# Shared memory region at a multiple of 128 bytes, step sizes computed behind the convolution, first transfers in another order

## What is computed

```python
def mamba2_mixer(u, w_in, conv_w, conv_b, dt_bias, a_log, d_skip, norm_g, w_out):
    b, l, _ = u.shape
    zxbcdt = u @ w_in
    z, xbc, dt = jnp.split(zxbcdt, [D_INNER, D_INNER + CONV_DIM], axis=-1)
    xbc = lax.conv_general_dilated(
        xbc, conv_w[:, None, :].astype(xbc.dtype), window_strides=(1,),
        padding=[(D_CONV - 1, 0)], dimension_numbers=('NWC', 'WIO', 'NWC'),
        feature_group_count=CONV_DIM)
    xbc = jax.nn.silu(xbc + conv_b)
    xs, bm, cm = jnp.split(xbc, [D_INNER, D_INNER + SSM_GROUPS * D_STATE], axis=-1)
    dt = jax.nn.softplus(dt.astype(jnp.float32) + dt_bias.astype(jnp.float32))
    a = -jnp.exp(a_log.astype(jnp.float32))
...
    y = ssd_chunked(xs, dt.reshape(b, l, SSM_GROUPS, SSM_HPG), a.reshape(SSM_GROUPS, SSM_HPG),
...
    y = y.reshape(b, l, D_INNER) * jax.nn.silu(z.astype(jnp.float32))
    y = grouped_rmsnorm(y, norm_g)
    return y.astype(u.dtype) @ w_out
```

## Time and profile before

| | us |
|---|---|
| three runs | 981.8, 981.83, 982.46 |
| median | 981.83 |
| profiled execution | 982.02 |
| its span, first to last instruction | 980.2 |
| mean granted TensorE clock | 0.983 of 2.4 GHz |
| TensorE busy | 927.5 (95%) |
| VectorE busy | 562.7 (57%) |
| ScalarE busy | 487.9 (50%) |
| read from memory | 162.01 MB, 166 GB/s over the span |

### The profile page before, as it was taken

The page is one execution under the profiler, slowest core; times in us unless marked ns, Lnnn a source line. Parts: engine busy times, 40 slices in busy tenths (PEclk is TensorE's granted clock), DMA queues, the critical chain, the costliest instruction groups (busy, mean ns, idle before and its releaser), DMA issues.

```text
span 980.2 us, 15470 instructions
## 1 busy us (share of the span) xinstructions
PE 927.5 (95%) x6560; PEld 855.4 (87%) x6560; DVE 562.7 (57%) x644; ACT 487.9 (50%) x669; POOL 37.3 (4%) x52
## 2 busy tenths in 40 slices
PE   2899998998999999999999999999999599999996
PEld 2899997876899889999988899997898499999885
DVE  4778654784475475455544755765654645554533
ACT  4555747773464564443343644665645534444332
POOL 1000001220000000000000021000000000000000
PEclk9899999998999999999999999999999799999999
DMA  9465553223464265555555697433543445555551
GB/s 294 141 194 187 172 173 109 88 86 131 170 221 166 86 215 172 178 195 183 172 188 198 197 275 236 131 129 123 198 152 98 139 133 193 188 171 175 201 181 43
DMA packets 120917, 163.80 MB, mean 167 GB/s; under 512 B 4060, under 2 KB 106644, under 8 KB 120868
## 3 DMA queue, kind: packets, MB, share of 16 engines
q1 hardware_dynamic: 117396, 151.47, 47.4%
q0 software_dynamic: 3472, 11.63, 4.0%
HBM read 162.01 MB, written 1.07 MB: 166 GB/s over the span
## 4 chain that ended last, share of the span: by engine, by line
PE 85%; DVE 7%; ACT 3%; DMA 2%; issue 2%; SPq 0%; POOL 0%; DVEq 0%
PE bank L433 77%; DMA w_raw<-in_ssm_w_in_dram 2%; DVE w_lo L1110 2%; DVE ntmp L1171 1%; PE bank L713 1%; PE bank L684 1%; DVE x L1174 1%; PE bank L533 1%; DVE ntmp L1150 1%; ACT ntmp L822 1%; PE bank L610 1%; PE bank L768 1%; DVE stats L1139 0%; DVE stats L1141 0%; PE bank L758 0%
## 5 line engine op out<-in xcount | busy, mean ns | idle before, releaser
L1110 DVE TENSOR_TENSOR w_lo<-w_raw,w_hi 128x2048 fp32r<-128x2048 f32 x136 | 310.8, 2290 | 229.2 <-ACT w_hi L802 229.1
L433 PE MATMUL bank<-actT_hi,w_hi 128*128 128x256 f32 x1280 | 365.5, 286 | 4.7 <-DVE dtc L1217 2.0
L433 PE MATMUL bank<-actT_lo,w_hi 128*128 128x256 f32 x1280 | 363.8, 284 | 0.0
L433 PE MATMUL bank<-actT_hi,w_lo 128*128 128x256 f32 x1280 | 363.6, 284 | 0.0
L802 ACT ACTIVATE w_hi<-w_raw 128x2048 fp32r<-128x2048 f32 x136 | 258.7, 1907 | 118.3 <-DMA w_raw<-in_ffn_w_down_dram 54.8
L433 PEld LDWEIGHTS bank<-actT_hi,w_hi 128*128 128x128 f32 x1280 | 247.3, 193 | 6.5 <-issue 4.2
L433 PEld LDWEIGHTS bank<-actT_lo,w_hi 128*128 128x128 f32 x1280 | 247.4, 193 | 0.1
L433 PEld LDWEIGHTS bank<-actT_hi,w_lo 128*128 128x128 f32 x1280 | 247.3, 193 | 0.0
L433 PE MATMUL bank<-w_lo,hT_hi 128*128 128x512 f32 x176 | 70.2, 399 | 0.0
L433 PE MATMUL bank<-w_hi,hT_hi 128*128 128x512 f32 x176 | 69.4, 394 | 0.0
L433 PE MATMUL bank<-w_hi,hT_lo 128*128 128x512 f32 x176 | 69.0, 392 | 0.0
(11 more groups left out here) (208 smaller groups left out, 1300.7 us busy)
## 6 DMA issues: line engine op xcount, KB each, us to landing
w_raw<-in_ffn_w_gu_dram SPq DMA_DIRECT2D x44, 1024.0 KB, 5.1
w_raw<-in_ffn_w_down_dram SPq DMA_DIRECT2D x22, 1024.0 KB, 4.9
w_raw<-in_ssm_w_in_dram SPq DMA_DIRECT2D x20, 1024.0 KB, 5.3
w_raw<-in_mem_w_kv_dram SPq DMA_DIRECT2D x16, 1024.0 KB, 5.6
w_raw<-in_ssm_w_out_dram SPq DMA_DIRECT2D x8, 1024.0 KB, 4.9
w_raw<-in_mem_w_q_dram SPq DMA_DIRECT2D x8, 1024.0 KB, 5.2
w_raw<-in_mem_w_o_dram SPq DMA_DIRECT2D x8, 1024.0 KB, 4.9
w_raw<-in_w_kv_dram SPq DMA_DIRECT2D x8, 1024.0 KB, 5.7
```

The lines of the kernel that those rows point to most:

```text
L433: ins = pe.matmul(dst, a, b, start=first and n == 0, stop=last and n == len(passes) - 1, skip_group_check=True)
L1110: dve.tensor_tensor(lo[:, s, :], raw[:, s, :], hi[:, s, :].bitcast(F32), ALU.subtract).then_inc(w_lo_done, 1)
```

## The change

Three things are changed together.

1. `phase` is rounded up to a multiple of 128 bytes (96 bytes later), and with it `scratch`. `dt_heads` moves to another place in the region.
2. The step sizes. The 24 products and the copy to `dt_heads` move behind `z0`, the two transposes behind `z1`, and the rest (bias, softplus, `dt_ready`) into the block of the memory statistics, which moves on ScalarE and VectorE from behind `z1` to behind `z2`. The convolution no longer waits for `dt_biased`. The step sizes use banks 6 and 7, the parameters' transposes bank 3, and `("dt", 0)` leaves the list of users of banks 0 and 1.
3. First transfers. SP issues x, `pre_row`, the first 128 columns of the constants (the identity for transposes, `ident_loaded`), unit 0, the small parameters, unit 1, the rest of the constants, units 2 and 3, and `dtw`. POOL waits for the first half of the normalised x before its small arrays, and for the third used unit before the next `pre_row`, `memV` and `post_row`. Unit 0 is split in two halves, so that VectorE begins after the first (`first_hi`), and ScalarE loads the SiLU table between units 0 and 1.

```diff
-BANKED = [("params", 0), ("dt", 0)] + [n for n in NAME_OF if KIND[n[0]] != "M"]
+BANKED = [("params", 0)] + [n for n in NAME_OF if KIND[n[0]] != "M"]
...
-        phase = at[0]
+        phase = -(-at[0] // 128) * 128
         PHASE = 49152
-        at[0] += PHASE
+        at[0] = phase + PHASE
...
-        dt_heads = place("dt_heads", [P, S], F32, phase)
+        dt_heads = place("dt_heads", [P, S], F32, phase + 44544)
...
@@ SP
-            sp.dma_start(const[:], A["consts"][:, 0:C_HOT]).then_inc(const_loaded, 16)
+            sp.dma_start(pre_row[:], every_row(TURN_GAIN[0])).then_inc(pre_first, 16)
+            sp.dma_start(const[:, 0:P], A["consts"][:, 0:P]).then_inc(ident_loaded, 16)
+            load(0)
             sp.wait_ge(par_cleared, 1)
...
-            sp.dma_start(dtw[:], row_tiles(w_in, 0, KD, DI + CONV, SSM_HEADS)).then_inc(par_loaded, 16)
-            for u in range(NUNITS):
+            load(1)
+            sp.dma_start(const[:, P:C_HOT], A["consts"][:, P:C_HOT]).then_inc(const_loaded, 16)
+            for u in range(2, SLOTS):
+                load(u)
+            sp.dma_start(dtw[:], row_tiles(w_in, 0, KD, DI + CONV, SSM_HEADS)).then_inc(dtw_loaded, 16)
+            for u in range(SLOTS, NUNITS):
                 load(u)
@@ POOL
-            pool.dma_start(pre_row[:], every_row(TURN_GAIN[0])).then_inc(pre_loaded, 16)
+            pool.wait_ge(u_ready, 1)
...
             pool.wait_ge(u_ready, 2)
+            pool.wait_ge(w_used, 3)
@@ TensorE
-            pe.wait_ge(const_loaded, 16)
+            pe.wait_ge(ident_loaded, 16)
             turn(0)
...
             u0 = U[("xbc", 0)]
-            pe.wait_ge(dt_biased, 1)
-            pe.wait_ge(t_out["dve"], 1)
             with pe.Fori(0, 3) as i:
...
-                banked("z", i, actT_hi, actT_lo, FREED[V_OF[("z", i)] - 4] if i < 2 else None)
+                banked("z", i, actT_hi, actT_lo, FREED[V_OF[("xbc", 9)]] if i < 2 else None)
+                if i == 0:
+                    steps()
+                if i == 1:
+                    steps_turned()
                 if i == 3:
+                    pe.wait_ge(dt_biased, 1)
                     turn(1)
@@ ScalarE
-            act.wait_ge(par_loaded, 80)
-            act.activation(dtw_hi[:], dtw[:], ACT.Copy).then_inc(dtw_hi_done, 1)
             turn(0, actT_hi)
+            hi_part(0, 0)
+            hi_part(0, 1)
+            act.preload_act_table_set("silu_and_others")
             hi_upto(1)
...
+            act.wait_ge(dtw_loaded, 16)
+            act.activation(dtw_hi[:], dtw[:], ACT.Copy).then_inc(dtw_hi_done, 1)
             for i in range(DI // TC):
                 hi_upto(U[("z", i)] + 2)
+                if i == 1:
+                    act.wait_ge(dt_mm, 1)
+                    act.activation(dt_heads[0:SSM_HEADS, :], bank[0:SSM_HEADS, 6, 0:S], ACT.Copy).then_inc(dt_copied, 1)
...
-                if i == 1:
+                if i == 2:
                     act.preload_act_table_set("natural_log_exp_and_others")
...
+                    act.wait_ge(dt_biased, 1)
+                    own.mark(act.activation(dtc[:, 2], dtc[:, 1], ACT.Abs))
...
@@ VectorE
-            dve.wait_ge(par_loaded, 80)
+            dve.wait_ge(par_loaded, 64)
...
+            turn(0, actT_hi, actT_lo)
+            lo_part(0, 0)
+            lo_part(0, 1)
...
+            lo_upto(1)
             dve.wait_ge(const_loaded, 16)
...
+            dve.wait_ge(dtw_hi_done, 1)
+            dve.tensor_tensor(dtw_lo[:], dtw[:], dtw_hi[:].bitcast(F32), ALU.subtract).then_inc(dtw_lo_done, 1)
             for i in range(DI // TC):
                 lo_upto(U[("z", i)] + 2)
-                if i == 1:
+                if i == 2:
+                    steps_biased()
                     for t in range(ST):
                         normalise(1, 2 + t, t, memV)
+                    steps_ready()
```

More of the change, by code:

```diff
@@ L539, in turn_done, with steps, steps_turned @@
                 pe.wait_ge(turn_lo, 4 * k + 4)
[L541 removed]
+            pe.wait_ge(ident_loaded, 16)
             turn(0)
[L544 removed]
             pe.wait_ge(consts_made, 1)
             for r in range(2):
[L547 removed]
+                ins = pe.transpose(bank[:, 3, r * P:(r + 1) * P], par_rows[:, r, :], ident)
             ins.then_inc(par_turned, 1)
             turn_done(0)
[L551 to L562 removed]
+            def steps():
+                pe.wait_ge(dtw_lo_done, 1)
+                for k in range(KD):
+                    ins = product(bank[0:SSM_HEADS, 6, 0:S],
+                                  [(dtw_hi[:, k, :], actT_hi[:, k, :]), (dtw_hi[:, k, :], actT_lo[:, k, :]), (dtw_lo[:, k, :], actT_hi[:, k, :])],
+                                  k == 0, k == KD - 1)
+                ins.then_inc(dt_mm, 1)
+            def steps_turned():
+                pe.wait_ge(dt_copied, 1)
+                for t in range(ST):
+                    ins = pe.transpose(bank[:, 7, t * SSM_HEADS:(t + 1) * SSM_HEADS], dt_heads[0:SSM_HEADS, t * P:(t + 1) * P],
+                                       ident[0:SSM_HEADS, 0:SSM_HEADS])
+                ins.then_inc(dt_turned, 1)
             u0 = U[("xbc", 0)]
[L566 to L567 removed]
             with pe.Fori(0, 3) as i:
@@ L810, in hi_part @@
                 ins = act.activation(hi[:, u % SLOTS, cols], raw[:, u % SLOTS, cols], ACT.Copy)
+                if u == 0 and part == 0:
+                    ins.then_inc(first_hi, 1)
                 if part:
@@ L885, in _ @@
                 statistic(t, t, x[:, t, :])
[L886 to L887 removed]
             turn(0, actT_hi)
+            hi_part(0, 0)
+            hi_part(0, 1)
+            act.preload_act_table_set("silu_and_others")
             hi_upto(1)
[L891 to L900 removed]
+            act.wait_ge(t_out["dve"], 1)
             def silu_conv(i, j):
@@ L1116, in lo_part @@
                 s = u % SLOTS
-                if part == 0:
+                if part == 0 and u:
                     dve.wait_ge(w_hi_done, u + 1)
+                elif u == 0:
+                    dve.wait_ge((first_hi, w_hi_done)[part], 1)
                 ins = dve.tensor_tensor(lo[:, s, cols], raw[:, s, cols], hi[:, s, cols].bitcast(F32), ALU.subtract)
@@ L1233, in _, with steps_biased @@
-            own.wait()
-            for t in range(ST):
-                ins = dve.scalar_tensor_tensor(out=adt3[:, t], in0=dtc[:, 5, t:t + 1, :].broadcast_to([P, 3, SSM_HEADS]), scalar=-1.0,
-                                               in1=dt_row[:, 1:2, :].broadcast_to([P, 3, SSM_HEADS]), op0=ALU.mult, op1=ALU.mult)
-            ins.then_inc(dt_ready, 1)
+            def steps_biased():
+                dve.wait_ge(dt_turned, 1)
+                dve.wait_ge(rows_loaded, 64)
+                own.mark(dve.memset(brows[:, S:3 * P], NEG))
+                bias_row = dt_row[:, 0:1, :].broadcast_to([P, ST, SSM_HEADS])
+                dt_raw = bank[:, 7, 0:ST * SSM_HEADS].rearrange("p (t h) -> p t h", t=ST)
+                dve.tensor_tensor(dtc[:, 1], dt_raw, bias_row, ALU.add).then_inc(dt_biased, 1)
@@ new lines, in steps_ready @@
+            def steps_ready():
+                dve.wait_ge(dt_logged, 1)
+                own.mark(dve.tensor_scalar(dtc[:, 5], dtc[:, 3], 1.0, None, ALU.add))
+                own.wait()
+                own.mark(dve.tensor_scalar(dtc[:, 6], dtc[:, 5], 1.0, None, ALU.subtract))
+                own.wait()
+                own.mark(dve.tensor_tensor(dtc[:, 6], dtc[:, 3], dtc[:, 6], ALU.subtract))
+                own.mark(dve.reciprocal(dtc[:, 2], dtc[:, 5]))
+                own.wait()
+                own.mark(dve.tensor_tensor(dtc[:, 6], dtc[:, 6], dtc[:, 2], ALU.mult))
+                own.wait()
+                own.mark(dve.tensor_tensor(dtc[:, 6], dtc[:, 6], dtc[:, 4], ALU.add))
+                own.wait()
+                own.mark(dve.scalar_tensor_tensor(out=dtc[:, 5], in0=dtc[:, 1], scalar=0.0, in1=dtc[:, 6], op0=ALU.max, op1=ALU.add))
+                own.wait()
+                own.mark(dve.tensor_scalar(dtc[:, 4], dtc[:, 5], 1e-30, None, ALU.max))
+                own.wait()
+                for t in range(ST):
+                    ins = dve.scalar_tensor_tensor(out=adt3[:, t], in0=dtc[:, 5, t:t + 1, :].broadcast_to([P, 3, SSM_HEADS]), scalar=-1.0,
+                                                   in1=dt_row[:, 1:2, :].broadcast_to([P, 3, SSM_HEADS]), op0=ALU.mult, op1=ALU.mult)
+                ins.then_inc(dt_ready, 1)
```

75 lines of the change are left out of this document (17 added, 58 removed).

## The result

The changed kernel takes 971.12 us (median of four runs, 970.18 to 971.55) against 982.14 (981.8 to 982.71) of the kernel before in the same comparison: 0.9886 times as long, 95% interval 0.9869 to 0.9903. The profiled execution has a span of 969.1, to be set beside 980.2.

The account below looks back on a forecast made before the run. Start-up was taken to bound the kernel until 27.63 us, TensorE after it. Terms -10.8 + 2.8 + 0.15 + 0.3 + 0.75 + 0.65 = -6.1 gave 975.9 us profiled, 975.7 against the median 981.83; range 972.5 to 979.0.

Parts of the forecast that it names:

- the moved region ... 0: Shared region starting at `phase`, moved 96 bytes to a multiple of 128: claimed no difference, 0 us.
- a gain that no row shows: Unpriced gain from the moved region, on the fast side of the forecast; chance 0.04.
- The start, -10.8: Start of the convolution on TensorE: at 16.8 us instead of 27.63, so -10.8 us.
- The low clock at the first unit: First convolution unit on TensorE: starts at the low clock, with the same 1.9 us of excess as before.
- The gate units, +4.65: Costs in the gate units: +2.8, +0.15, +0.3, +0.75 and +0.65 us.
- the step work: Between gate units on TensorE: 24 step products +2.8, wait for `dtw_lo` +0.15, two transposes +0.3 us.
- the turn: Memory transposes behind z3: the second eight wait for the second normalisation, +0.75 us.
- z5: Behind z4 and the cumulative sums, TensorE waits for the low part of unit 17: +0.65 us.
- 2: Rival at the start: transfers no earlier than before, unit 1 split only at 27.2; total 978.2 us; chance 0.13.
- 4: Rival at the start: units arrive over 5.76 us apart, first units run at low clock; 987.4 with two; chance 0.04.
- 3 (a costlier block): Rival on ScalarE's longer block: splits of units 17 and 18 each 1.5 us later; total 978.9; chance 0.12.
- 1 (a high clock at the start): Rival at the convolution's start: clock high at 16.8 or better timed, taking off 1.9 us; total 973.8; chance 0.12.

Follow-up runs that it names:

- `b_align`: Kernel before with one edit, the shared region's start rounded up to a multiple of 128 bytes; 975.25 us against 982.05 (0.993).
- `warm_start`: `act32r` plus 14 unread identity transposes before the first weights, and parameter rows made between the halves of `actT_lo`; 958.86 us (0.9761).
- `act32r`: Changed kernel with `actT` and `memT` moved on by 32 bytes and everything behind them by 1024 in all; 961.11 us (0.9788).

## Why the prediction was wrong, step by step

**The step that failed** is "the moved region ... 0". It priced the region by ScalarE's copies into it, 598 against 598 ns. ScalarE writes there; TensorE reads there, in 816 products of 512 columns, and those rows were not looked at. They were in the trace of before: two output products of one shape, 72 in the chain, took 16.37 with `actT` and 17.01 with `oT`, which lies in the region. 17.01 - 16.37 over 72 is 0.009, times 816 is 7 us. That is too much, since 0.2 of the 0.64 stays when the region is moved (16.57 against 16.38). The real figure is 4.9 from the paces. The totals give 5.7 (976.82 to 971.12) and 6.8 (982.05 to 975.25); the second has `b_align`'s earlier start in it. "A gain that no row shows" was given 0.04; a row did show it.

**The start, -10.8.** Right in mechanism: 17.31 for 16.8, so -10.3. The 0.5 is VectorE's wait for `d_pair` until 12.25, a transfer issued behind unit 0, which the sum did not price: ScalarE's second half at 15.42 and VectorE's 1.26 behind it would have made the 16.8. In `warm_start` the wait is gone; its start is 0.47 earlier than `act32r`'s (17.77 to 17.30), 0.29 of which is an earlier landing of `pre_row`. The low clock at the first unit was forecast and came, 4.6 us of it where 3.9 was assumed: another 0.4. The 0.107 that the prediction sets beside the step products' 0.118 is in no row; rows 2 and 8 give 0.120 for 256 columns at 2.4 GHz, which makes its argument on the clock no weaker.

**What the start was due to** was told only in part. The text named `dt_heads` behind unit 1 and unit 1 behind its transfer, and cured both. It did not ask what curing one would leave: order alone gives as much as both.

**The gate units, +4.65.** The memory's turn starts at 115.09 where it was 121.74: 10.0 has become 6.65, so the step work cost 3.4 (3.25 in the sum). TensorE's next product is 5.5 ahead instead: 1.1 for the turn (0.75), its second half having waited 0.73. At 150 us 4.94 is left: 0.6 for z5 (0.65). In sum 5.1.

**Rivals.** Units came in time (unit 1 was split from 16.73, TensorE waited 0.3 us for a unit once), which rules out 2 and 4. 3 (a costlier block) was worth 0.3, not 3. 1 (a high clock at the start) did not happen by itself and was worth 1.9 when made to. The late low stretch, 13.5 us, moved with the program and nearly kept its length.

So by its own rows the forecast was 1.2 too fast up to 150 us (4.94 for 6.1), and 6.1 too slow behind it. Of these 6.1 the region's products are 4.9; the rest is for the greater part the clock, at its lower level for 1.8 us less in the product with y (0.9).

## What to carry to other kernels

Where a change moves a tile, look at every engine that reads it, and first at the one that bounds the kernel: compare two groups of the same shape that differ only in where their operand lies. Where two causes stand in line before a wait, price each cure with the other already made. And an idle bound engine has a second price, the clock of what follows; cheap work in the gap bought 1.9 and 3.2 us here.

## What the runs showed of the hardware

The pace of a TensorE product of 32-bit operands depended on the distance of its operands' starts, with 256 and 512 bytes like 0: 0.1133 to 0.1200 us for 256 columns, 0.230 to 0.236 for 512 with `oT` stationary (16.56 to 17.01 for 72), with opposite tastes. At 64 and 192 bytes products of 256 columns had two paces, 0.1134 and 0.1178, that changed from stage to stage. The data were the same throughout. Start addresses alone were worth up to 1.4% of this kernel (971.1 to 957.4, the second a single execution), and no idle time in the profile points to it. Float32 transposes of the identity, 14 in the gap before the first weights, had the products behind them start at 2.4 GHz instead of 1.2.
